# A second modulation on VectorE alone: weights laid with outputs on partitions, one multiply-and-add-up step for each column of outputs

## The chip, the cores and the metric

The kernel runs on one core of one Trainium2 chip (trn2). The core has TensorE (matrix products into PSUM), VectorE, ScalarE, GpSimd, SyncE (which here only issues DMAs), an on-chip memory of 128 partitions (SBUF), and PSUM in eight banks of 512 fp32 columns. The engines run their own instruction streams and wait for one another through semaphores. The metric is the device time of one execution in microseconds (us); lower is better.

## The reference

Two transformer blocks run one after the other on 512 tokens of width 1024, all in fp32. What matters here is the first lines of the first block: a condition vector `c` gives, by one product with a 1024 x 6144 matrix, the six vectors that shift, scale and gate both halves of the block.

```python
s_lat = jax.nn.silu(c)                                   # c: (1, 1024)
mod_l = (s_lat @ w_mod[l] + b_mod[l])[:, None, :]        # w_mod: (1024, 6144)
sh1, sc1, g1, sh2, sc2, g2 = jnp.split(mod_l, 6, axis=-1)
h = _modulate(_rms(x, norm1_g[l]), sh1, sc1)             # needs sh1, sc1 at once
p = h @ w_in[l]                                          # queries, keys, Fourier input, gates ga, gb
...
x = x + g1 * _merge(p, attn_lat, four_lat, ...)          # g1 much later
h2 = _modulate(_rms(x, norm2_g[l]), sh2, sc2)            # sh2, sc2 before the experts
x = x + g2 * _expert_choice(h2, *moe_w)
```

`sh1` and `sc1` are the first modulation. The other four vectors, 4096 outputs of 1024 products each (16 MB of weights), are the second modulation, and are needed only from the merge after the attention on.

## The kernel before

Channels lie on the 128 partitions in 8 groups (KD), tokens along the free axis. A projection tile is one PSUM bank: 128 outputs by 512 tokens, over 8 groups of inputs. Each product is made of three passes (L988 to L990, function `mm3`): both factors are split into a high part (`w_hi`, `h_hi`) and the rest (`w_lo`, `h_lo`), and high x high, high x low and low x high are added up in PSUM. So a tile is 24 matrix products.

Weights come as one stream of chunks, [128, 2048] fp32, 1 MB each. SyncE loads them in a fixed order into a ring of four `raw` slots (L804, L832 to L842). Split chunks are converted by ScalarE (`w_hi`, L1817) and then by GpSimd in two halves (`w_lo`, L918 and L920) into a ring of three; the last of these steps frees the raw slot (`w_lo_done`). A refill waits until the chunk four places before it is done with, and the refills wait in order, so one late slot holds the whole ring. The first section (s1) has 19 split chunks of 16 blocks of 128 x 128 weights, numbered 0 to 18; TensorE takes its blocks in order: queries, keys, Fourier, then gates `ga` (blocks 115 to 178) and `gb` (179 to 242), then `four_o`. Chunk 11 starts at block 176, the sixth block of tile ga 7.

The 16 chunks of the second modulation (raw chunks, not split) are put into this stream by `MOD_BEHIND`: one behind each of split chunks 8 and 9, two behind each of 10 to 16. A chunk holds two groups of 128 outputs, with inputs on the partitions: for output group m and input group k a 128 x 128 block. VectorE works through it in `modulation_b` (L2259): the first step (L2269) scales the k = 0 blocks by the condition (one number for each partition, `csil`), seven more (L2271) multiply and add on, each over 2 x 128 elements, with the running sum in PSUM bank 7; the last writes it into `macc` in SBUF and frees the raw slot (`macc_done`). What is left is a sum over partitions. TensorE does that in `mod_b_tile` (L1020): two products with `macc` as weights and a column of ones, in one of six turning PSUM banks; `mod_b_evac` (L2254) on VectorE adds the bias and writes two columns of `mod`. These tiles stand in TensorE's hand-written order behind ga 4 to 7, gb 0 to 7 and four_o 0 to 3 (L1217 to L1238).

VectorE starts on the second modulation when it is done with the rotated and normalised query rows (`q_rows`, L2443), which also free the PSUM banks for the `ga` tiles. `mod` is first needed (`modb_done`, L1400) at the router logits after the attention.

Of the kernel before, what the change touches and what calls it, by code (L numbers as in the profile page):

```python
# [8 lines left out]
ALU = mybir.AluOpType  # L9
# [279 lines left out]
def make_plan():  # L289
# [37 lines left out]
    for j in range(KD):  # L327
        p.add("ga", j, by="act", split=blocks(s1, S1_GA + j * 8 * B, 8))
        if j >= 4:
            p.add("mod_b", j - 4, by=("modb_done", j - 3))  # L330
    for j in range(KD):
        p.add("gb", j, by="act", split=blocks(s1, S1_GB + j * 8 * B, 8))
        p.add("mod_b", 4 + j, by=("modb_done", 5 + j))
# [4 lines left out]
    for j in range(KD // 2):  # L338
        four_o(j)
        p.add("mod_b", 12 + j, by=("modb_done", 13 + j))  # L340
# [158 lines left out]
def build(nc, stream, cols_d, x_d, ctx_d, router_d, wab_d, rope_t_d, dftc_d, ident_d, iota_d, xt_d, out):  # L499
    with ExitStack() as ctx:  # L500
# [76 lines left out]
        macc = at("macc", R + 104, [P, 4, 2, B])  # L577
# [96 lines left out]
        def ex(m):  # L674
# [28 lines left out]
        macc_done = sem("macc_done")  # L703
# [78 lines left out]
                   "modb_done": modb_done, "silu_e": silu_e, "act_t_done": act_t_done,  # L782
# [18 lines left out]
        def _(sp):  # L801
# [30 lines left out]
            def refill(n):  # L832

                split, k = CHUNKS[n - NRAW]
                if split:
                    sp.wait_ge(w_lo_done, k + 1)
                else:
                    sp.wait_ge(macc_done, k + 1)
# [119 lines left out]
        def _(pe):  # L958
# [52 lines left out]
            def mod_tile(g):  # L1011
# [6 lines left out]
                done(last)  # L1018

            def mod_b_tile(k):  # L1020

                o = open_tile("mod_b", k)
                pe.wait_ge(macc_done, k + 1)
                for m in range(2):
                    last = mm(o[:, m:m + 1], macc[:, k % 4, m, :], one, start=True, stop=True)  # L1025
# [210 lines left out]
            for j in range(KD // 2):  # L1236
                four_out(j)
                mod_b_tile(12 + j)  # L1238
# [561 lines left out]
        def _(act):  # L1800
# [102 lines left out]
            for g in range(NF):  # L1903
                hi(f_hi[:, g, :], take("f", g))
            for g in range(NF + 1):
# [7 lines left out]
                if g >= 1:  # L1913
# [5 lines left out]
                    hi(f_hi[:, g - 1, :], four_f[:, g % 2, :])  # L1919
            for half in range(2):  # L1920
# [298 lines left out]
        def _(dve):  # L2219
# [34 lines left out]
            def mod_b_evac(k):  # L2254
                m = 16 + 2 * k
                V.tensor_tensor(mod[:, m:m + 2, 0], take("mod_b", k)[:, 0:2], col("b_mod", m, 2), ALU.add)\
                    .then_inc(modb_done, 1)

            def modulation_b(c):  # L2259
# [3 lines left out]
                if c < 2:  # L2263
                    dve.wait_ge(qtok_done, 2 * TT)
                else:
                    dve.wait_ge(macc_done, c - 1)
                w = raw[:, n % NRAW, :].rearrange("p (m k c) -> p m k c", m=2, k=KD)
                acc = psum[:, 7, c % 2 * 2 * B:(c % 2 + 1) * 2 * B].rearrange("p (m c) -> p m c", m=2)
                link(V.tensor_scalar(acc, w[:, :, 0, :], csil[:, 0:1], None, ALU.mult))  # L2269
                for k in range(1, KD):  # L2270
                    ins = V.scalar_tensor_tensor(out=acc if k < KD - 1 else macc[:, c % 4, :, :], in0=w[:, :, k, :],  # L2271
                                                 scalar=csil[:, 2 * k:2 * k + 1], in1=acc, op0=ALU.mult, op1=ALU.add)
                    if k < KD - 1:
                        link(ins)
                ins.then_inc(macc_done, 1)

# [196 lines left out]
            for c in range(5, 12):  # L2473
                mod_b_evac(c)
                if c + 4 < 16:
                    modulation_b(c + 4)
# [7 lines left out]
            for j in range(KD // 2):  # L2484
                four_gate(j)
                mod_b_evac(12 + j)
# [641 lines left out]
```

## Time and profile before

| what | us |
|---|---|
| median of 3 runs | 1310.37 (1309.72 to 1312.95) |
| the profiled execution's own time | 1308.97 |
| its span, first to last instruction | 1307.2 |
| TensorE busy in the span | 1290.0 |
| VectorE busy | 675.6 |
| ScalarE busy | 472.1 |
| GpSimd busy | 447.4 |
| mean granted TensorE clock | 0.995 of full |

The profile is of one execution. PE is TensorE, DVE VectorE, ACT ScalarE, POOL GpSimd, SP SyncE. A busy TensorE need not be at its peak: matrix products overlap, and their ends are modelled, so the distance between two starts says more than a duration. Idle time of an engine that nothing waits for costs nothing. The second modulation lies between 149 and 235 us.

### The profile page before, as it was taken

The page shows a single profiled execution, that of the slowest core. Times are in us where ns is not written, and L with a number is a line of the kernel's source. Part 1 is how long each engine was busy: PE and PEld are TensorE (multiplying, and loading weights), DVE is VectorE, ACT ScalarE, POOL GpSimd, SP SyncE. Part 2 cuts the span into 40 slices and gives each one's busy share as a digit, 9 for nine tenths or more (in the row PEclk, how much of TensorE's full clock was granted, in tenths as well). Part 3 has the DMA queues.
Part 4 walks back from the last instruction along what each step waited for, and adds up shares of the span by engine and source line. Part 5 has one row for each costly group of instructions (what it writes and reads, how often), then busy time and mean ns, then how long its engine had stood idle before and what let it go on. Part 6 is the DMA issues. An engine that isn't in the chain of part 4 may idle for free.

```text
span 1307.2 us, 15683 instructions
## 1 busy us (share of the span) xinstructions
PE 1290.0 (99%) x6240; PEld 951.9 (73%) x6240; DVE 675.6 (52%) x1262; ACT 472.1 (36%) x640; POOL 447.4 (34%) x215
## 2 busy tenths in 40 slices
PE   8999999999999999999999999999999999999998
PEld 5789888866588734443357788888888888888887
DVE  2467987668873634342258557422551551551553
ACT  4354232356541312111154661433431431431443
POOL 3153254157630100000035243544254444444440
PEclk9999999999999899999999999999999999999999
DMA  9522298201027899999963221332123223223101
GB/s 374 226 98 97 99 355 303 80 3 63 33 101 298 316 423 420 420 420 420 421 262 119 96 98 65 108 118 97 60 102 123 72 97 124 69 96 125 68 1 65
DMA packets 33764, 226.54 MB, mean 173 GB/s; under 512 B 3872, under 2 KB 4512, under 8 KB 7712
## 3 DMA queue, kind: packets, MB, share of 16 engines
q1 hardware_dynamic: 32256, 218.79, 43.4%
q0 software_dynamic: 1152, 4.19, 0.9%
q10 hardware_dynamic: 288, 2.62, 0.5%
q8 instruction: 46, 0.75, 0.2%
q14 instruction: 22, 0.18, 0.0%
HBM read 221.40 MB, written 4.19 MB: 173 GB/s over the span
## 4 chain that ended last, share of the span: by engine, by line
PE 93%; DMA 3%; DVE 2%; ACT 1%; issue 0%; POOL 0%; SPq 0%; DVEq 0%
PE psum L988 24%; PE psum L989 23%; PE psum L990 23%; PE psum L1531 11%; DMA ex_more<-in_stream 2%; PE psum L1302 2%; PE psum L1273 1%; DMA x<-in_x 1%; PE psum L1616 1%; PE psum L1491 1%; PE psum L1516 1%; DVE x L2613 1%; PE psum L1519 0%; PE psum L1007 0%; PE psum L1025 0%; PE psum L1258 0%
## 5 line engine op out<-in xcount | busy, mean ns | idle before, releaser
L918 POOL TENSOR_TENSOR w_lo<-raw,w_hi 128x1024 fp32r<-128x1024 f32 x79 | 190.4, 2410 | 569.0 <-ACT w_hi L1817 567.6
L988 PE MATMUL psum<-b_hi,w_hi 128*128 128x512 f32 x608 | 238.1, 392 | 0.1
L990 PE MATMUL psum<-b_hi,w_lo 128*128 128x512 f32 x608 | 236.7, 389 | 0.0
L989 PE MATMUL psum<-b_lo,w_hi 128*128 128x512 f32 x608 | 236.6, 389 | 0.0
L1817 ACT ACTIVATE w_hi<-raw 128x2048 fp32r<-128x2048 f32 x80 | 152.6, 1907 | 143.2 <-PE psum L990 101.9
L920 POOL TENSOR_TENSOR w_lo<-raw,w_hi 128x1024 fp32r<-128x1024 f32 x79 | 191.3, 2422 | 0.0
L988 PEld LDWEIGHTS psum<-b_hi,w_hi 128*128 128x128 f32 x608 | 114.1, 188 | 30.8 <-issue 5.7
L990 PEld LDWEIGHTS psum<-b_hi,w_lo 128*128 128x128 f32 x608 | 114.1, 188 | 24.1
L989 PEld LDWEIGHTS psum<-b_lo,w_hi 128*128 128x128 f32 x608 | 114.2, 188 | 23.1
L1531 PE MATMUL psum<-ex_ring,xe 128*64 128x512 f32 x432 | 95.0, 594 | 0.0
L2611 DVE TENSOR_TENSOR x<-psum,x 128x512 f32<-128x512 f32 x39 | 26.9, 692 | 127.7 <-PE psum L990 127.7
L988 PE MATMUL psum<-h_hi,w_hi 128*128 128x512 f32 x200 | 81.1, 406 | 1.3 <-POOL w_lo L900 1.3
L990 PE MATMUL psum<-h_hi,w_lo 128*128 128x512 f32 x200 | 78.2, 391 | 0.0
L989 PE MATMUL psum<-h_lo,w_hi 128*128 128x512 f32 x200 | 78.0, 390 | 0.0
L988 PE MATMUL psum<-ff_hi,w_hi 128*128 128x512 f32 (+1 forms) x198 | 75.9, 383 | 0.0
L990 PE MATMUL psum<-ff_hi,w_lo 128*128 128x512 f32 (+1 forms) x198 | 75.7, 383 | 0.0
L989 PE MATMUL psum<-ff_lo,w_hi 128*128 128x512 f32 (+1 forms) x198 | 75.7, 383 | 0.0
L2927 DVE TENSOR_TENSOR psum<-psum,rstd_s 128x512 f32<-128x512 f32 x48 | 33.5, 697 | 77.4 <-PE psum L990 77.4
L1531 PEld LDWEIGHTS psum<-ex_ring,xe 128*64 128x64 f32 x432 | 30.3, 137 | 59.0 <-issue 58.6
L930 POOL DMA_INDIRECT xg<-xt,ids x8 | 9.2, 1152 | 180.8 <-PE psum L1519 127.1
L2613 DVE SCALAR_TENSOR_TENSOR x<-psum,mod,x 128x512 f32<-128x512 f32 x72 | 50.5, 744 | 26.4 <-PE psum L990 20.1
L2810 DVE TENSOR_TENSOR act_r<-psum,gate_s 128x512 f32<-128x512 f32 x8 | 5.5, 692 | 86.2 <-PE psum L1531 86.2
(463 smaller groups left out, 2349.0 us busy)
## 6 DMA issues: line engine op xcount, KB each, us to landing
raw<-in_stream SPq DMA_DIRECT2D x97, 1024.0 KB, 4.8
ex_ring<-in_stream SPq DMA_DIRECT2D x78, 1024.0 KB, 20.4
ex_more<-in_stream SPq DMA_DIRECT2D x18, 1024.0 KB, 21.6
mod_in<-in_stream SPq DMA_DIRECT2D x8, 1024.0 KB, 20.8
x<-in_x SPq DMA_DIRECT2D x4, 512.0 KB, 6.5
x<-in_x ACTq DMA_DIRECT2D x1, 2048.0 KB, 7.5
xt<-h2t SPq DMA_DIRECT2D x8, 256.0 KB, 9.5
out<-y_out SPq DMA_DIRECT2D x4, 512.0 KB, 3.0
```

Of the source, the lines that this page charges most:

```text
L918: nc.gpsimd.tensor_tensor(w_lo[:, slot, w], raw[:, raw_slot, w], w_hi[:, slot, w].bitcast(F32), ALU.subtract)
L920: nc.gpsimd.tensor_tensor(w_lo[:, slot, w], raw[:, raw_slot, w], w_hi[:, slot, w].bitcast(F32), ALU.subtract).then_inc(w_lo_done, 1)
L988: mm(o, w[0], x[0], start=start, stop=False)
L989: mm(o, w[0], x[1], start=False, stop=False)
L990: return mm(o, w[1], x[0], start=False, stop=stop)
L1273: done(mm(o[:, 0:KH], q_hi[b][0:QK, q * P:(q + 1) * P], k_hi[b][0:QK, s * KH:(s + 1) * KH], start=True, stop=True))
L1302: last = mm(psum[s * VD:s * VD + VD, 6 + h % 2, :], v[:, k + s, h * VD:h * VD + VD], probs[k + s][:], start=k == 0, stop=k == KT - 2)
L1531: last = mm(o[e * CAP:(e + 1) * CAP, :], x_of(k, e), w[:, (2 * (k - k0) + e) * T:(2 * (k - k0) + e + 1) * T], start=k == 0, stop=k == ks - 1)
L1817: A(w_hi[:, c % NHL, :], raw[:, n % NRAW, :], ACT.Copy).then_inc(w_hi_done, 1)
L2611: ins = V.tensor_tensor(x1[:, j, :], o, x1[:, j, :], ALU.add)
L2613: ins = V.scalar_tensor_tensor(out=x1[:, j, :], in0=o, scalar=scale, in1=x1[:, j, :], op0=ALU.mult, op1=ALU.add)
L2927: V.tensor_tensor(o, o, rstd, ALU.mult).then_inc(ffz_done, 1)
```

## The change

The chunks of the second modulation are laid out anew on the host: outputs on partitions, and along the free axis the 1024 weights of each output; a chunk still holds two groups of 128 outputs. The condition is loaded once as a [128, 1024] array with the same row on every partition (`c_rows`), and ScalarE takes its silu there. VectorE then does each group of 128 outputs in one step that multiplies by this row, adds up along the free axis, starts from the bias, and writes one column of `mod`. The `mod_b` tiles of TensorE, their evacuation and `macc` go. `c_rows` takes the place of `macc` in SBUF; `k_rows` lies in the same bytes before, so the load waits for the `kr` tile that reads it.

```diff
 # plan: no mod_b tiles
     for j in range(KD):
         p.add("ga", j, by="act", split=blocks(s1, S1_GA + j * 8 * B, 8))
-        if j >= 4:
-            p.add("mod_b", j - 4, by=("modb_done", j - 3))
...
-        macc = at("macc", R + 104, [P, 4, 2, B])
+        c_rows = at("c_rows", R + 104, [P, D])
...
 # SyncE, refill of a slot that held a modulation chunk
-                    sp.wait_ge(macc_done, k + 1)
+                    sp.wait_ge(modb_done, k + 1)
...
 # TensorE
             for j in range(KD):
                 done(project(open_tile("ga", j), s1, S1_GA + j * 8 * B, B, ks, hx))
-                if j >= 4:
-                    mod_b_tile(j - 4)
             for j in range(KD):
                 done(project(open_tile("gb", j), s1, S1_GB + j * 8 * B, B, ks, hx))
-                mod_b_tile(4 + j)
...
 # ScalarE
             for g in range(NF):
                 hi(f_hi[:, g, :], take("f", g))
+                if g == 2:
+                    full(act, "kr")
+                    act.dma_start(c_rows[:], c_rows_d).then_inc(c_rows_in, 16)
...
+            act.wait_ge(c_rows_in, 16)
+            A(c_rows[:], c_rows[:], ACT.Silu).then_inc(c_rows_done, 1)
...
 # VectorE, modulation_b(c)
-                w = raw[:, n % NRAW, :].rearrange("p (m k c) -> p m k c", m=2, k=KD)
-                acc = psum[:, 7, c % 2 * 2 * B:(c % 2 + 1) * 2 * B].rearrange("p (m c) -> p m c", m=2)
-                link(V.tensor_scalar(acc, w[:, :, 0, :], csil[:, 0:1], None, ALU.mult))
-                for k in range(1, KD):
-                    ins = V.scalar_tensor_tensor(out=acc if k < KD - 1 else macc[:, c % 4, :, :], in0=w[:, :, k, :],
-                                                 scalar=csil[:, 2 * k:2 * k + 1], in1=acc, op0=ALU.mult, op1=ALU.add)
...
+                w = raw[:, n % NRAW, :].rearrange("p (m i) -> p m i", m=2)
+                for i in range(2):
+                    m = 16 + 2 * c + i
+                    ins = V.tensor_tensor_reduce(out=w[:, i, :], in0=w[:, i, :], in1=c_rows[:], scale=1.0, scalar=col("b_mod", m),
+                                                 op0=ALU.mult, op1=ALU.add, accum_out=mod[:, m, 0:1])
+                ins.then_inc(modb_done, 1)
...
             for half in range(2):
                 q_sums(half)
                 q_rows(half)
-            for c in range(4):
-                modulation_b(c)
-            for c in range(5):
-                mod_b_evac(c)
-                modulation_b(c + 4)
...
+            dve.wait_ge(c_rows_done, 1)
+            for c in range(16):
+                modulation_b(c)
```

TensorE's order, at the end of tile ga 4, before:

```order
678 L989 MATMUL psum<-h_lo,w_hi 128x512
679 L990 MATMUL psum<-h_hi,w_lo 128x512
680 L1025 MATMUL psum<-ones,macc 128x1 [waits macc_done,qtok_done]
681 L1025 MATMUL psum<-ones,macc 128x1
682 L988 MATMUL psum<-h_hi,w_hi 128x512 [waits freed_act]
683 L989 MATMUL psum<-h_lo,w_hi 128x512
```

and now (the three passes have lines 985 to 987 in the changed file):

```order
678 L986 MATMUL psum<-h_lo,w_hi 128x512
679 L987 MATMUL psum<-h_hi,w_lo 128x512
680 L985 MATMUL psum<-h_hi,w_hi 128x512 [waits qtok_done]
681 L986 MATMUL psum<-h_lo,w_hi 128x512
682 L987 MATMUL psum<-h_hi,w_lo 128x512
```

The two one-column products and their wait for VectorE are gone; ga 5 follows ga 4 directly.

VectorE's order, from the last step of the query rows on, before (`small` holds the condition's silu, one number for each partition):

```order
193 L2462 TENSOR_TENSOR q_tok_111<-q_tok_111,r_q 128x4x32
194 L2269 TENSOR_SCALAR psum<-raw,small 128x256 [waits qtok_done,raw_full1]
195 L2271 SCALAR_TENSOR_TENSOR psum<-raw,small,psum 128x256 [waits dve_seq] x6
196 L2271 SCALAR_TENSOR_TENSOR macc<-raw,small,psum 128x256 [waits dve_seq]
197 L2269 TENSOR_SCALAR psum<-raw,small 128x256 [waits qtok_done,raw_full3]
198 L2271 SCALAR_TENSOR_TENSOR psum<-raw,small,psum 128x256 [waits dve_seq] x6
```

and now (ISA is the multiply-and-add-up step, and behind it the readout of the sum into a column of `mod`):

```order
193 L2439 TENSOR_TENSOR q_tok_111<-q_tok_111,r_q 128x4x32
194 L2251 ISA raw,mod<-raw,c_rows,cols 128x1024 [waits raw_full1,c_rows_done]
195 L2251 ISA mod 128x1
196 L2251 ISA raw,mod<-raw,c_rows,cols 128x1024
197 L2251 ISA mod 128x1
198 L2251 ISA raw,mod<-raw,c_rows,cols 128x1024 [waits raw_full3]
```

Eight steps for a chunk have become two with their readouts; the operands `raw` and `c_rows` are both in SBUF, where the second tensor was in PSUM.

ScalarE's order at the end of the Fourier stage, now (before, the rows are the same but for row 62):

```order
59 L1812 ACTIVATE f_hi<-four_f 128x512 [waits four_done]
60 L1903 ACTIVATE four_sin<-psum 128x256 [waits tile_full]
61 L1812 ACTIVATE f_hi<-four_f 128x512 [waits four_done]
62 L1909 ACTIVATE c_rows<-c_rows 128x1024 [waits c_rows_in]
63 L1802 ACTIVATE w_hi<-raw 128x2048 [waits raw_full0,tile_full]
64 L1916 ACTIVATE sqs_q<-psum 128x384 [waits tile_full] x2
65 L1916 ACTIVATE sqs_q<-psum 128x384 [waits qsum_done,tile_full] x6
```

The silu of `c_rows` has been put ahead of a weight split and of the squares of the query rows, without a table load beside it.

## Rows read from the trace of the kernel before

**Rows 1.** The page, busy time (us, share of the span) and instructions.

```profile
PE 1290.0 (99%) x6240; PEld 951.9 (73%) x6240; DVE 675.6 (52%) x1262; ACT 472.1 (36%) x640; POOL 447.4 (34%) x215
```

**Rows 2.** TensorE's waits for a weight split: us in total, times, longest.

```profile
PE psum L988 <- POOL w_lo L900: 1.3, 2, 0.9
```

**Rows 3.** Timeline of TensorE, first products behind each tile: start us, us.

```profile
144.80 0.39 PE L988 MATMUL psum<-h_hi,w_hi 128*128 128x512 f32 x1
...
150.24 0.39 PE L988 MATMUL psum<-h_hi,w_hi 128*128 128x512 f32 x1
...
155.68 0.50 PE L1025 MATMUL psum<-ones,macc 128*128 128x1 f32 x4
...
161.63 0.50 PE L1025 MATMUL psum<-ones,macc 128*128 128x1 f32 x4
```

**Rows 4.** Two stretches: length, busy us of each engine, clock, DMA share, GB/s.

```profile
150.00:235.00 85.00, 85.00 (x405) 70.85 (x404) 64.90 (x147) 21.08 (x21) 33.27 (x14) 1.00 0.83 309
...
525.00:660.00 135.00, 133.31 (x625) 54.70 (x622) 46.79 (x81) 22.08 (x47) 2.80 (x3) 1.00 1.01 421
```

**Rows 5.** VectorE, timeline of modulation chunk 0; last, line 2271's durations (ns).

```profile
149.20 0.49 DVE L2269 TENSOR_SCALAR psum<-raw,small 128x256 f32<-128x256 f32 x1
...
152.87 0.48 DVE L2271 SCALAR_TENSOR_TENSOR macc<-raw,small,psum 128x256 f32<-128x256 f32 x1
153.27 0.48 DVE L2269 TENSOR_SCALAR psum<-raw,small 128x256 f32<-128x256 f32 x1
...
L2271 DVE SCALAR_TENSOR_TENSOR psum<-raw,small,psum x96: 487/490/491, 149.7 to 224.9; 128x256 f32<-128x256 f32 x96
```

**Rows 6.** Timelines: chunk 11's conversion, TensorE's use, chunk 12's last half.

```profile
164.32 1.92 ACT L1817 ACTIVATE w_hi<-raw 128x2048 fp32r<-128x2048 f32 x1 [13.28 <-DMA raw<-in_stream]
...
168.66 2.40 POOL L920 TENSOR_TENSOR w_lo<-raw,w_hi 128x1024 fp32r<-128x1024 f32 x1
...
171.48 0.39 PE L988 MATMUL psum<-h_hi,w_hi 128*128 128x512 f32 x1
...
177.30 2.40 POOL L920 TENSOR_TENSOR w_lo<-raw,w_hi 128x1024 fp32r<-128x1024 f32 x1
```

**Rows 7.** SyncE, timeline: the refills from modulation chunk 0's release on.

```profile
153.38 4.87 SPq L805 DMA_DIRECT2D raw<-in_stream  x4
```

**Rows 8.** VectorE, groups by form: busy us, mean ns of one, idle.

```profile
L2940 DVE TENSOR_TENSOR ff_pre<-acc_u,ff_gl 128x512 f32<-128x512 f32 x24 | 16.6, 692 | 0.8
...
L2658 DVE SCALAR_TENSOR_TENSOR b_lo<-x,cols,b_hi 128x512 fp32r<-128x512 f32 x16 | 12.0, 750 | 0.8 <-ACT b_hi L1827 0.3
...
L2902 DVE TENSOR_TENSOR_SCAN lru_v<-lru_a,lru_b 128x512 f32<-128x512 f32 x8 | 11.9, 1484 | 0.3
...
L2511 DVE TENSOR_TENSOR k_tok<-kr_tok,r_k 128x256 f32<-128x256 f32 x6 | 2.5, 416 | 0.0
...
L2256 DVE TENSOR_TENSOR mod<-psum,cols 128x2 f32<-128x2 f32 x16 | 2.5, 154 | 5.7 <-PE psum L1025 5.7
```

**Rows 9.** Timelines: GpSimd's split steps and VectorE's steps on SBUF operands.

```profile
142.04 2.39 POOL L918 TENSOR_TENSOR w_lo<-raw,w_hi 128x1024 fp32r<-128x1024 f32 x1 [1.50 <-ACT w_hi L1817]
...
142.52 2.06 DVE L2462 TENSOR_TENSOR q_tok<-q_tok,r_q 128x128 f32<-128x128 f32 x1
...
114.93 2.10 DVE L2234 TENSOR_TENSOR f_lo<-four_f,f_hi 128x512 fp32r<-128x512 f32 x1 [0.77 <-ACT f_hi L1827]
...
116.44 2.86 POOL L920 TENSOR_TENSOR w_lo<-raw,w_hi 128x1024 fp32r<-128x1024 f32 x1
```

**Rows 10.** ScalarE 1024 wide; timelines around the first query rows and ga 0.

```profile
L1864 ACT ACTIVATE w_hi<-raw x1: 1057/1057/1057, 18.4 to 18.4; 128x1024 fp32r<-128x1024 f32 x1
...
122.40 0.49 ACT L1926 ACTIVATE sqs_q<-psum 128x384 f32<-128x384 f32 x1 [0.56 <-PE psum L990]
...
127.77 0.28 DVE L2462 TENSOR_TENSOR q_tok<-q_tok,r_q 128x128 f32<-128x128 f32 x1
...
128.44 0.39 PE L988 MATMUL psum<-h_hi,w_hi 128*128 128x512 f32 x1
```

More of the change, by code:

```diff
@@ L328, in make_plan @@
         p.add("ga", j, by="act", split=blocks(s1, S1_GA + j * 8 * B, 8))
-        if j >= 4:
-            p.add("mod_b", j - 4, by=("modb_done", j - 3))
     for j in range(KD):
         p.add("gb", j, by="act", split=blocks(s1, S1_GB + j * 8 * B, 8))
-        p.add("mod_b", 4 + j, by=("modb_done", 5 + j))
     def four_o(j, bank=None):
@@ L339, in make_plan @@
         four_o(j)
-        p.add("mod_b", 12 + j, by=("modb_done", 13 + j))
     for t in range(KT):
@@ L496, with build @@
 FFN_CHUNKS = 9
-def build(nc, stream, cols_d, x_d, ctx_d, router_d, wab_d, rope_t_d, dftc_d, ident_d, iota_d, xt_d, out):
+def build(nc, stream, cols_d, x_d, ctx_d, router_d, wab_d, rope_t_d, dftc_d, ident_d, iota_d, c_rows_d, xt_d, out):
     with ExitStack() as ctx:
@@ L702, in build @@
         cpad_zero = sem("cpad_zero")
-        macc_done = sem("macc_done")
+        c_rows_in = sem("c_rows_in")
+        c_rows_done = sem("c_rows_done")
         modb_done = sem("modb_done")
@@ L781, in build @@
                    "pre_done": pre_done, "accg_done": accg_done, "accu_done": accu_done,
-                   "modb_done": modb_done, "silu_e": silu_e, "act_t_done": act_t_done,
+                   "silu_e": silu_e, "act_t_done": act_t_done,
                    "rcol_done": rcol_done, "lru_b_done": lru_b_done, "gcol_done": gcol_done}
@@ L1017, in mod_tile @@
                               start=True, stop=True)
[L1018 to L1025, printed above, removed]
                 done(last)
@@ L1237, in _ @@
                 four_out(j)
-                mod_b_tile(12 + j)
             def token_rows(o, t, off):
@@ L2252, in mod_evac @@
                 dve.wait_ge(freed_dve, PLAN.freed_count(TILE["mod", g]))
[L2254 to L2257, printed above, removed]
             def modulation_b(c):
@@ L2467, in _ @@
                 q_rows(half)
-            for c in range(4):
+            dve.wait_ge(c_rows_done, 1)
+            for c in range(16):
                 modulation_b(c)
-            for c in range(5):
-                mod_b_evac(c)
-                modulation_b(c + 4)
[L2473 to L2476, printed above, removed]
             def four_gate(j):
@@ L2485, in _ @@
                 four_gate(j)
-                mod_b_evac(12 + j)
             V.memset(k_hi[0][QK:QK + 1, :].bitcast(F32), 1.0)
@@ L3033 @@
              for q in range(4) for base in (0, D) for k in range(KD)]
-    mod = tiles(w_mod)[:, 8 * CH:]
+    mod = w_mod[:, 2 * D:].T.reshape(-1, P, D).transpose(1, 0, 2).reshape(P, -1)
     w_in = a["w_in"][0]
@@ L3118 @@
               "rope_t": rope_t, "dftc": dftc, "ident": np.eye(P, dtype=f),
-              "iota": np.ascontiguousarray(iota)}
+              "iota": np.ascontiguousarray(iota),
+              "c_rows": np.ascontiguousarray(np.broadcast_to(a["c"][0].reshape(1, D), (P, D)))}
     nc = bacc.Bacc("TRN2", target_bir_lowering=False, num_devices=1)
```

7 lines of the change are left out of this document (removed).

## The prediction

> **What bounds the kernel now.** I read the busy shares first. TensorE is busy 1290.0 of 1307.2 us [rows 1], so a change counts only as far as it removes TensorE work or makes TensorE wait. TensorE's list of waits comes next: no weight chunk is waited for after the first one [rows 2] (L900 is the first chunk's split alone). Then the table by stretches: in 150 to 235 us, where the second modulation runs, TensorE is busy all 85.00 us at granted clock 1.00 (2.4 GHz), VectorE 64.90 and GpSimd 33.27 us, and the DMA engines carry 309 GB/s [rows 4]. So the stretch is TensorE's, with three suppliers close behind, and these have to be followed one by one.
>
> **What goes from TensorE.** A plain projection tile, 24 matrix products, takes 150.24 - 144.80 = 5.44 us from start to start. With a mod_b tile behind it the period is 161.63 - 155.68 = 5.95 us [rows 3]. One mod_b tile (two one-column products, in the trace four) therefore costs 0.51 us, more than its columns suggest, since the products behind it start slowly as well. Sixteen of them, the last four behind shorter tiles but of the same form: 8.1 us, all on the path.
>
> **What goes from and comes to VectorE.** Before, a chunk takes 153.27 - 149.20 = 4.07 us: eight steps of 256 elements in a chain [rows 5]. Now it takes two multiply-and-add-up steps of 1024 elements, each followed by a readout of one column (the piece of VectorE's order, now). The trace has no such step, so I bound it. A two-input step on SBUF operands takes 692 ns for 512 elements and 416 for 256, that is 1.08 ns for one element, hence 692 + 512 x 1.08 = 1.24 us for 1024 [rows 8]. Its successor starts 0.08 us before its recorded end, as in rows 5 (0.48 us long, next start 0.40 later). So T = 1.16 us, or 1.2 by the three-input form (750 ns). The upper end is the scan, also a running result over two inputs: 1484 ns for 512 [rows 8], so up to 2.97 us. The lower end is 1.11 us, the slope alone. I take 1.16, because the form is that of the two-input step and the scan feeds each result into the next product, while a sum does not have to; the readout I take as 0.1 us, between nothing and the 0.15 us of a step on two columns [rows 8]. A chunk is then 2 x 1.26 = 2.5 us, and VectorE has 16 x 1.5 = 24 us less to do; that by itself is off the path and worth nothing.
>
> The Trainium skill speaks against this change. "Vector Engine (DVE) Microarchitecture Reference", section "Points that are easy to get wrong", says that this family of steps runs at half throughput with two SBUF sources that aren't bf16, as no read port is left for the accumulator. The rows show 750 ns for such a step with two fp32 SBUF sources and 512 elements [rows 8], which is no halving; but that step adds nothing up, so the rule isn't refuted. By the rule a step would take some 2.3 us and the kernel about 1327 us (rival 2, worked out there from rows), by the row 1.2 and 1303.
>
> **The weight ring.** A raw slot is handed back when its modulation chunk is done, and SyncE's queue refills in order. The row of SyncE at 153.38 is the refill that waited for mod chunk 0; it and three more go out within 4.87 us [rows 7]. The third of them is weight chunk 11 of the first section, and ScalarE starts on it at 164.32 [rows 6], 10.9 us after 153.38: three transfers of 1.05 MB at 309 GB/s [rows 4] are 10.2 us. So this burst is held by the DMA rate, and only its start can be moved. GpSimd ends the chunk's low part at 168.66 + 2.40 = 171.06, and TensorE first uses it at 171.48 (tile ga 7, block 5) [rows 6]. That is a cushion of 0.42 us, which the waits list doesn't show. After the change three mod_b tiles fewer stand ahead of it, so TensorE wants it at 171.48 - 1.53 = 169.95. VectorE is done with chunk 0 at 149.20 + 2.5 = 151.7 instead of 153.3, so the burst starts 1.6 us earlier: ScalarE starts at 162.7, GpSimd at 164.7. Without more, the low part would be ready at 169.4, in time.
>
> **The shared port.** Here the new step's operands count. The old steps had their second tensor in PSUM, and all 96 took 487 to 491 ns [rows 5], whatever GpSimd did. Steps of VectorE with both tensors in SBUF don't: one of 128 elements, started at 142.52, ends at 144.58 with GpSimd's step 142.04 to 144.43; the other way round GpSimd's step from 116.44 takes 2.86 us instead of 2.40, as VectorE's from 114.93 had waited and held it until 117.03 [rows 9]. So they exclude one another, and a waiting VectorE step goes first at the change-over. (The Trainium skill, "SBUF — State Buffer", section "Who interferes with whom", has this as a lock held for the whole instruction when VectorE has two SBUF inputs and GpSimd reads SBUF; by that rule each of the 32 new steps can block half a weight split. The trace agrees.) Mod chunk 4 is the fourth transfer of the burst and lands at about 165, inside GpSimd's first half (164.7 to 167.1). Its first step waits until 167.1 and runs to 168.3; GpSimd's second half follows, to 170.7. TensorE, wanting it at 169.95, waits 0.8 us.
>
> Behind that the ring has room. One round is a weight chunk of 16 blocks, 2 x 5.44 = 10.9 us of TensorE, and holds two mod chunks and one split. With everything on the port in turn it needs 4 x (T + 0.1) + 4.7 = 9.7 us. Chunk 12 was ready at 177.30 + 2.40 = 179.7 [rows 6] with TensorE's need at 171.48 + 2 x 5.95 = 183.4; after, the need is 181.6 (five tiles fewer, 0.8 later), and the split starts about 1.6 us earlier, takes up to two steps (2.4 us) more, and is ready at about 180.5. I see no second wait.
>
> **The added conversion of the condition.** The DMA (0.5 MB) goes out behind the third f tile and is wanted behind the last Fourier tile, with the whole Fourier stage in between; covered. The Silu over 1024 elements takes about 1.0 us by the nearest row (1057 ns) [rows 10]; no table load stands with it in its order. It stands ahead of a split and of the squares of the query rows. Of these, the fourth waited for TensorE 0.56 us [rows 10], and VectorE's sums follow it, so some 0.4 us of the 1.0 reach the query rows. VectorE frees the first bank at 127.77 + 0.28 = 128.05, and TensorE takes it at 128.44 [rows 10]: the 0.4 us use up that cover, and 0.1 us may show. Later the same lag vanishes: the step from 142.52 waits for GpSimd until 144.4 anyway [rows 9], so modulation still starts at 149.2. Were that cover gone, the first wait grows by the 0.4.
>
> The PSUM banks turn over in another order without mod_b, but each bank still comes back after six tiles (33 us) until the fixed ones. mod is needed at the logits, hundreds of us later.
>
> **Sum.** -8.1 + 0.8 + 0.1 = -7.2 us. The profiled execution took 1308.97 us (span 1307.2, 1.8 around it), 1.4 below the median of 1310.37. So its counterpart is 1301.8, and the median forecast 1303.2. Without the lock it would be -8.1; with T of 1.45 chunk 11 comes 1.5 to 2 us late, and it is about -6.
>
> **The rivals.**
> 1. *The forecast*, 1303.2 (1302 to 1305): 0.65.
> 2. *Two cycles for one element.* T is then 0.14 + 2 x 1.08 x 1024 ns = 2.35 us, and a round needs 4 x 2.45 + 4.7 = 14.5 us against 10.9. The burst starts 0.8 us later, GpSimd begins at 167.1 and, with two steps of 2.35 in between, ends at 176.5: chunk 11 is 6.5 us late. The rounds of chunks 13 to 17 lose 3.6 each (that of 12 lies in the first wait): 6.5 + 18 - 8.1 = +16.4, about 1327 us. At the scan's 2.97 a round loses 6.0 and the time is about 1341. It decides from T = 1.45, where the round is full; at about 1.8 us the whole gain is gone. For it: the scan's row. Against it: the sum needs no feedback. 0.10.
> 3. *The lock costs more than one step*, by T of 1.5 to 1.7, by a readout that takes the port too, or by GpSimd losing each turn: waits of 1 to 3 us at chunk 11 and about 1 at later chunks, gain 1 to 5 us, about 1307. 0.15.
> 4. *The gain is given back in the expert stage*, where the DMA engines are busy to a share of 1.01 from 525 to 660 us [rows 4]. For it: a stream that ran from a fixed time would end when it did. Against it: it starts on slots that TensorE's progress frees, so it starts as much earlier. 1310. 0.08.
> 5. The rest, 0.02: something else, of either sign.
>
> What can be told from no change is 0.3%, 3.9 us, so 1306.4 and 1314.3 are the bounds. Case 1 and half of case 3 are faster: 0.73. Half of case 3, case 4 and a little of 5 are the same: 0.16. Case 2 and the rest are slower: 0.11. The range 1301.5 to 1309 takes in case 1 and most of case 3, about 0.8; the likeliest case's own range is 1302 to 1305.
>
> **What would show it.** Right: a step of 1.2 to 1.3 us x32 on VectorE; tile periods of 5.44 us through gb; a single wait of TensorE for a weight split, 0.3 to 1.5 us long near 170 us; some GpSimd halves of 3.5 us instead of 2.4; everything behind 235 us earlier by one amount. Wrong: steps above 1.45 us, waits on the splits at every second or third tile, or a shift at 235 us that is smaller by 650 us.

## The result, and the profile after

| | before | after |
|---|---|---|
| median, us (4 runs each, alternating on one chip) | 1310.05 (1309.65 to 1312.95) | 1301.09 (1299.18 to 1302.03) |
| profiled execution, us | 1308.97 | 1301.71 |
| its span | 1307.2 | 1299.9 |
| mean granted TensorE clock | 0.995 | 0.996 |

The ratio is 0.992 (0.9907 to 0.9934): faster by 9.0 us. Forecast were 7.2 us and 1303.2 us, with a range from 1301.5. The direction and the main term were right; the time lies 0.4 us below the range.

The page after, busy time (compare [rows 1]):

```profile
PE 1282.9 (99%) x6176; PEld 945.6 (73%) x6176; DVE 671.2 (52%) x1182; ACT 473.3 (36%) x641; POOL 453.3 (35%) x215
```

TensorE is busy 7.1 us less, with 64 products fewer, and still 99% of the span. The stretch of the second modulation (length, busy us of each engine, clock, DMA share, GB/s; compare [rows 4]):

```profile
150.00:235.00 85.00, 85.00 (x376) 70.25 (x375) 67.54 (x80) 25.19 (x26) 45.48 (x16) 1.00 0.81 310
525.00:660.00 135.00, 131.70 (x614) 53.34 (x611) 42.77 (x73) 23.69 (x48) 6.53 (x4) 1.00 1.01 421
```

TensorE is still busy throughout. VectorE is shown busy 67.54 us where it was 64.90, though its work was to fall by some 24 us, and GpSimd 45.48 where it was 33.27. Part of this is work of the next stage that now falls into the window: 16 halves of weight splits on GpSimd instead of 14, and some 6 us more on VectorE. The rest is told by the groups and the timelines. VectorE's groups from 145 to 245 us (busy us, mean ns of one, idle before):

```profile
L2251 DVE CUSTOM_DVE_ANT_0 raw<-raw,c_rows,cols 128x1024 f32<-128x1024 f32 x32 | 58.3, 1872 | 11.5 <-DMA raw<-in_stream 11.5
...
L2251 DVE DVE_READ_ACCUMULATOR2_ANT mod<- 128x1 f32 x32 | 2.5, 78 | 0.0
```

VectorE's timeline (start us, us), first where GpSimd is idle, then at modulation chunk 4:

```profile
150.23 1.28 DVE L2251 CUSTOM_DVE_ANT_0 raw<-raw,c_rows,cols 128x1024 f32<-128x1024 f32 x1
151.44 0.08 DVE L2251 DVE_READ_ACCUMULATOR2_ANT mod<- 128x1 f32 x1
151.44 1.28 DVE L2251 CUSTOM_DVE_ANT_0 raw<-raw,c_rows,cols 128x1024 f32<-128x1024 f32 x1
...
165.03 3.05 DVE L2251 CUSTOM_DVE_ANT_0 raw<-raw,c_rows,cols 128x1024 f32<-128x1024 f32 x1 [2.47 <-DMA raw<-in_stream]
168.01 0.07 DVE L2251 DVE_READ_ACCUMULATOR2_ANT mod<- 128x1 f32 x1
168.01 3.41 DVE L2251 CUSTOM_DVE_ANT_0 raw<-raw,c_rows,cols 128x1024 f32<-128x1024 f32 x1
```

GpSimd's timeline over the same chunks:

```profile
164.60 2.40 POOL L915 TENSOR_TENSOR w_lo<-raw,w_hi 128x1024 fp32r<-128x1024 f32 x1 [17.32 <-ACT w_hi L1802]
166.96 3.37 POOL L917 TENSOR_TENSOR w_lo<-raw,w_hi 128x1024 fp32r<-128x1024 f32 x1
173.50 2.59 POOL L915 TENSOR_TENSOR w_lo<-raw,w_hi 128x1024 fp32r<-128x1024 f32 x1 [3.17 <-ACT w_hi L1802]
```

By itself the step takes 1.28 us and the next starts 1.21 us after it; the readout (0.08 us) lies beside the next step. The step that starts at 165.03 takes 3.05 us, since GpSimd's half, 164.60 to 167.00, is under way; GpSimd's second half then takes 3.37 us instead of 2.40, as VectorE goes first at the change-over; and VectorE's next step, begun inside that half, takes 3.41. Both engines are shown busy while they wait for each other. In e3 below, where they don't, the same 32 steps are busy 39.6 us instead of 58.3. So 18.7 us of VectorE's time here is waiting.

ScalarE starts on chunk 11 of the first section, and TensorE uses it (two timelines; compare [rows 6]):

```profile
162.60 1.92 ACT L1802 ACTIVATE w_hi<-raw 128x2048 fp32r<-128x2048 f32 x1 [11.13 <-DMA raw<-in_stream]
```

```profile
170.17 0.39 PE L987 MATMUL psum<-h_hi,w_lo 128*128 128x512 f32 x1
170.40 0.48 PE L985 MATMUL psum<-h_hi,w_hi 128*128 128x512 f32 x1
170.72 0.40 PE L986 MATMUL psum<-h_lo,w_hi 128*128 128x512 f32 x1
```

GpSimd is done at 166.96 + 3.37 = 170.33, and TensorE takes the chunk at 170.40, where its turn comes anyway. TensorE's list has no wait for a split in this stretch; the next product starts 0.32 us later instead of 0.23, and this 0.1 us is all that the chunk costs.

ScalarE starts 1.72 us earlier than before (162.60 for 164.32). The refill behind modulation chunk 0 goes out only 0.63 us earlier, and the other 1.1 us come behind it. SyncE's refills before, each line with two, and the DMA engines (last two numbers: share, GB/s) between 160 and 162 us:

```profile
153.38 0.80 SPq L805 DMA_DIRECT2D raw<-in_stream  x2
157.44 0.81 SPq L805 DMA_DIRECT2D raw<-in_stream  x2
160.00:162.00 2.00, 2.00 (x13) 1.69 (x12) 1.90 (x4) 0.00 (x0) 0.00 (x0) 1.00 0.80 250
```

and after:

```profile
152.75 0.80 SPq L802 DMA_DIRECT2D raw<-in_stream  x2
155.17 0.80 SPq L802 DMA_DIRECT2D raw<-in_stream  x2
160.00:162.00 2.00, 2.00 (x10) 1.67 (x9) 2.00 (x5) 0.00 (x0) 0.00 (x0) 1.00 0.98 414
```

The third refill, chunk 11's, waits for VectorE to hand back modulation chunk 1. With 4.07 us for a chunk it goes out at 157.44, and the DMA rate has a gap at 160 us; with 2.42 us it goes out at 155.17, and there is no gap.

A sharper measure than the windows is how much later or earlier the same product of TensorE starts, taken over all its products in order, without the one-column ones. The first product on the latent keys starts here in the kernel before and in the kernel after:

```profile
234.37 0.49 PE L988 MATMUL psum<-w_hi,ckv_hi 128*128 128x512 f32 x1
```

```profile
226.95 0.39 PE L985 MATMUL psum<-w_hi,ckv_hi 128*128 128x512 f32 x1
```

They are 7.42 us apart. The same difference at other places, against the kernel before's first profile (us; b1_before is a second profile of the kernel before, a1_after one more of the kernel after):

| at (before's time) | after | a1_after | b1_before |
|---|---|---|---|
| 150 | +0.44 | +0.46 | +0.51 |
| 240 | -7.56 | -7.48 | +0.51 |
| 420 | -7.49 | -7.55 | +0.43 |
| 450 | -7.85 | -9.02 | +0.79 |
| 700 | -7.24 | -8.10 | +1.47 |

Between 150 and 240 us both profiles of the kernel after gain 7.9 to 8.0 us. The second execution of the kernel before is 0.5 us later from 20 us on, and 1.5 us later at 700.

### The profile page after: what moved, and what is told of

Its sections match the earlier page's. It is cut to its first block, busy times and chain, and to the rows that moved or that the text cites. A ratio compares the mean times of both kernels' runs of the same rounds, so it can differ in the third digit from the quotient of the medians.

```text
span 1299.9 us, 15446 instructions
## 1 busy us (share of the span) xinstructions
PE 1282.9 (99%) x6176; PEld 945.6 (73%) x6176; DVE 671.2 (52%) x1182; ACT 473.3 (36%) x641; POOL 453.3 (35%) x215
## 4 chain that ended last, share of the span: by engine, by line
PE 93%; DMA 4%; DVE 2%; SPq 1%; ACT 0%; issue 0%; DVEq 0%
PE psum L985 24%; PE psum L986 23%; PE psum L987 23%; PE psum L1516 11%; DMA ex_more<-in_stream 2%; PE psum L1287 2%; DMA mod_in<-in_stream 2%; PE psum L1258 1%; PE psum L1601 1%; DVE x L2583 1%; PE psum L1476 1%; PE psum L1501 0%; PE psum L1504 0%; PE psum L1243 0%; PE psum L1029 0%; PE psum L1004 0%
## 5 line engine op out<-in xcount | busy, mean ns | idle before, releaser
L915 POOL TENSOR_TENSOR w_lo<-raw,w_hi 128x1024 fp32r<-128x1024 f32 x79 | 192.0, 2430 | 555.7 <-ACT w_hi L1802 554.3
L917 POOL TENSOR_TENSOR w_lo<-raw,w_hi 128x1024 fp32r<-128x1024 f32 x79 | 197.2, 2496 | 0.0
L2251 DVE CUSTOM_DVE_ANT_0 raw<-raw,c_rows,cols 128x1024 f32<-128x1024 f32 x32 | 58.3, 1872 | 11.5 <-DMA raw<-in_stream 11.5
```

What stands on the lines that cost most here:

```text
L915: nc.gpsimd.tensor_tensor(w_lo[:, slot, w], raw[:, raw_slot, w], w_hi[:, slot, w].bitcast(F32), ALU.subtract)
L917: nc.gpsimd.tensor_tensor(w_lo[:, slot, w], raw[:, raw_slot, w], w_hi[:, slot, w].bitcast(F32), ALU.subtract).then_inc(w_lo_done, 1)
L2251: ins = V.tensor_tensor_reduce(out=w[:, i, :], in0=w[:, i, :], in1=c_rows[:], scale=1.0, scalar=col("b_mod", m), op0=ALU.mult, op1=ALU.add ...
```

## The experiments

**The kernel after once more, and the columns back.** a1_after is the kernel after without an edit. e1_columns_back adds at each of the 16 places:

```diff
+            def column_products():
+                pe.wait_ge(qtok_done, 2 * TT)
+                for m in range(2):
+                    mm(psum[:, 7, 510 + m:511 + m], ident[:], one, start=True, stop=True)
```

> The changed kernel as it is, timed again beside the kernel before, to size the gain. Theory A (only TensorE's sixteen column tiles count): 16 x 0.505 = 8.1 us go, a wait of 0.1 for weight chunk 11 and 0.1 for the late first query rows come: 8.0 us faster, ratio 0.9939, and the 9.0 us of the first comparison are partly scatter between executions. Theory B (something behind 235 us gives another us, in the expert stage or by the clock): 9 us or more again, ratio 0.9932 or less.

> The changed kernel with two one-column products put back at each of the sixteen places in TensorE's order; they multiply the identity by a column of ones into a spare corner of bank 7, nothing waits for them and nothing reads them. Theory A: the whole gain goes, within 0.5 us of the kernel before (ratio 0.9995 to 1.0005). Theory B, or a gain that comes from VectorE's shorter work: it stays at least 1 us faster.

Measured: a1_after 1301.29 (1300.68 to 1301.54), ratio 0.9919 (0.9906 to 0.9932). e1_columns_back 1312.10 us, ratio 1.000 (0.9992 to 1.0009). By its time a1_after speaks for theory B, as it is 10.2 us faster than the kernel before in the same comparison; in the stage it gains the 8.0 us of theory A. What lies between is taken up at the end. Against the profile after, e1's later products start 0.08 us later at 150 and 8.07 at 235, in steps of 0.5 us. With the 32 short products back (64 in the trace), and VectorE, GpSimd and the ring as after, the whole gain is gone. The gain is TensorE's time; e9 below shows what VectorE's shorter work adds.

**How many columns.** The same with one product (e7) and four (e8) at each place.

```diff
-                for m in range(2):
+                for m in range(1):      # e8: range(4), columns 508 to 511
```

> The kernel after, with one one-column product (instead of two) at each of the 16 places where a mod_b tile stood; its result is not used. Two cost 0.50 us for each place by the shift of TensorE's later products (8.07 us for 16). Theory A, each product pays for itself (its own weights have to be brought in, and one column is too short to hide that): about 0.25 us a place, 4 us in all, 1305.3 us. Theory B, the cost is that of breaking into the run of 512-column products, whatever stands there: 0.4 to 0.45 us a place, 6.5 to 7 us, about 1308 us.

> The same with four one-column products at each of the 16 places. Theory A: about 1.0 us a place, 16 us in all, so about 1317 us, unless the suppliers' added time hides nothing (TensorE is the bound there, so all of it shows). Theory B: 0.6 to 0.7 us a place, 10 to 11 us, about 1312 us.

Measured: e7 1305.77 us, ratio 0.9953 (0.9936 to 0.9969); e8 1316.49 us, ratio 1.0039 (1.0027 to 1.005). The shift from 150 to 235 us was 3.83 us (0.24 a place) for one product, 7.99 (0.50) for two and 15.14 (0.95) for four. Timeline of TensorE in e8:

```profile
156.13 0.95 PE L1210 MATMUL psum<-ones,ident 128*128 128x1 f32 x8
156.94 0.49 PE L985 MATMUL psum<-h_hi,w_hi 128*128 128x512 f32 x1
157.27 0.40 PE L986 MATMUL psum<-h_lo,w_hi 128*128 128x512 f32 x1
157.50 0.40 PE L987 MATMUL psum<-h_hi,w_lo 128*128 128x512 f32 x1
```

The four (eight in the trace) hold the engine for 156.94 - 156.13 = 0.81 us, and the product behind them is followed after 0.33 instead of 0.23 us. The price grows with the number of products, about 0.24 us for each fp32 product of one column. That is theory A's count; its reason, the weights that each product brings in, was not tested by itself. A pass of 512 columns has a pitch of 5.44 / 24 = 0.23 us, so a one-column product costs about as much.

**Before without the tiles.** VectorE keeps its eight steps; the sum over partitions is left out. In e2 the small step that writes `mod` reads `macc` in SBUF; e9 reads PSUM instead for chunks 0 to 11.

```diff
-                mod_b_tile(j - 4)            # and at the other 12 places
...
-                V.tensor_tensor(mod[:, m:m + 2, 0], take("mod_b", k)[:, 0:2], ...)
+                dve.wait_ge(macc_done, k + 1)
 # e2
+                V.tensor_tensor(mod[:, m:m + 2, 0], macc[:, k % 4, :, 0], ...)
 # e9
+                part = psum[:, 7, (k + 1) % 2 * 2 * B:(k + 1) % 2 * 2 * B + 2] if k < 12 else macc[:, k % 4, :, 0]
+                V.tensor_tensor(mod[:, m:m + 2, 0], part, ...)
```

> The kernel before with the mod_b tiles taken from TensorE and nothing else: VectorE still does eight steps a chunk, and its evacuation takes one column of the running sums instead of their sum over partitions (that sum is left out, so the modulation's values are other ones). Theory A: -8.1 us for the tiles, but weight chunk 11 is ready at 171.1 as before and wanted at 169.95: a wait of 1.1 us appears for it, so 7.0 us faster, ratio 0.9947, 1 us less than the changed kernel. If VectorE's shorter work is worth nothing at all: 8.1 faster and no wait.

> Before without the sixteen mod_b tiles, like e2_no_tiles (the sum over partitions is left out), but the small step that writes two columns of mod has its first operand in PSUM for chunks 0 to 11, as the old evacuation had. In e2_no_tiles both its operands lay in SBUF, and it took 1131 ns on average instead of 154 (18.1 us instead of 2.5), so VectorE there had some 15 us more to do than before the change. Theory A, the 2.7 us between e2 and the kernel after were an artefact of these steps: about 1301.5 us, and TensorE waits neither for gbf nor for the split by more than 0.5 us near 230 us. Theory B, VectorE's eight steps for each chunk are themselves too long once TensorE runs 8 us ahead: about 1303 to 1304 us with waits of 1.5 to 3 us left at that place.

Measured: e2 1304.04 us (1302.38 to 1307.18), ratio 0.994 (0.9926 to 0.9955); e9 1303.29 (1301.33 to 1306.15), ratio 0.9944 (0.9931 to 0.9958). TensorE's waits in 145 to 245 us (us in total, times, longest), in e2 and then in e9:

```profile
PE psum L984 <- DVE gbf L2475: 2.6, 2, 2.2
PE psum L984 <- POOL w_lo L916: 1.0, 1, 1.0
```

```profile
PE psum L984 <- POOL w_lo L916: 0.9, 1, 0.9
```

And VectorE's group that differs, in e2:

```profile
L2249 DVE TENSOR_TENSOR mod<-macc,cols 128x2 f32<-128x2 f32 x16 | 18.1, 1131 | 0.0
```

A step on two columns takes 1131 ns on average there against 154 ns with an operand in PSUM [rows 8], since half of them start beside one of GpSimd's halves and wait for its end (0.15 us alone, 1.25 to 2.39 us beside one). That delays VectorE until TensorE waits for `gbf`. So e2 was spoilt in part by its own edit. In e9 the wait for `gbf` is gone and one of 0.9 us is left, at chunk 11; the shift from 150 to 240 us is -6.9 against -8.0 for the whole change. This is what VectorE's shorter work is worth, 0.9 us of waiting and 1.1 in the shift: with the long steps ScalarE takes chunk 11 at 164.41, as before, and with the short ones at 162.60, and the chunk comes in time. At the end of the stage, where theory B expected waits, there are none, yet the time is the one of theory B. By the medians e9 is 2.2 us behind the kernel after, but its runs scatter over 4.8 us, so about 1 us is shown and the rest isn't explained.

**The port, with the row in PSUM.** ScalarE copies the silu of the row into PSUM banks 6 and 7 when they are free, behind ga 2, and the step reads it there.

```diff
+                if j == 2:                       # ScalarE, behind ga 2
+                    act.wait_ge(qtok_done, 2 * TT)
+                    A(c_ps, c_rows[:], ACT.Copy).then_inc(c_rows_done, 1)
...
-                        in1=c_rows[:], ...
+                        in1=c_ps, ...
```

> The changed kernel with the condition's row copied by ScalarE into PSUM banks 6 and 7 behind the query rows, and read from there. Theory of the shared port: all 32 steps take 1.28 us and all split halves of GpSimd 2.4 (none of 3.4), where now steps of 2 to 3.4 us and halves of 3.4 stand. As that lock costs TensorE only 0.1 us at chunk 11 in the changed kernel, the time is the same within 0.3 us. If the lock costs more than the trace's waits show (rival 3): 0.5 to 1 us faster than the changed kernel.

Measured: 1302.34 us, ratio 0.9929 (0.9916 to 0.9941). VectorE's group and GpSimd's in 145 to 245 us:

```profile
L2256 DVE CUSTOM_DVE_ANT_0 raw<-raw,psum,cols 128x1024 f32<-128x1024 f32 x32 | 39.6, 1279 | 25.8 <-DMA raw<-in_stream 24.7 <-ACT psum L1923 1.2
```

```profile
L918 POOL TENSOR_TENSOR w_lo<-raw,w_hi 128x1024 fp32r<-128x1024 f32 x9 | 21.7, 2408 | 0.0
L916 POOL TENSOR_TENSOR w_lo<-raw,w_hi 128x1024 fp32r<-128x1024 f32 x8 | 19.2, 2399 | 48.8 <-ACT w_hi L1803 48.8
```

Every step takes 1.28 us and every half 2.40: with one of VectorE's two tensors in PSUM the engines don't exclude each other, and VectorE's busy time falls from 58.3 to 39.6 us. (The Trainium skill, "SBUF — State Buffer", section "Who interferes with whom", names two SBUF inputs as the condition; e3 is the counterpart to the kernel after, and agrees.) Yet the time doesn't fall; it is 1.05 us above that of a1_after. The edit has a price of its own: VectorE waits 1.16 us for ScalarE's copy and starts on the modulation at 150.80. Chunk 11 is ready at 167.55 + 2.40 = 169.95 and is used at 170.01, 0.28 us behind its turn. So e3 doesn't price the exclusion exactly. What bounds its cost in the kernel after is that kernel's own timeline, 0.1 us at chunk 11: the rest was inside the suppliers' slack.

e3 also tells what held the burst. Its first refill goes out at 153.32, as before the change (153.38), and with the short steps ScalarE has chunk 11 at 163.20 all the same, 1.1 us sooner than before.

**The same work twice.** Each step is done twice, which gives steps of about 2.5 us, first with both tensors in SBUF (e4), then with the row in PSUM (e5).

```diff
+                    link(V.tensor_tensor_reduce(out=c_ps, in0=w[:, i, :], in1=c_rows[:], ...,   # e4
+                                                accum_out=mod[:, m, 1:2]))
                     ins = V.tensor_tensor_reduce(out=w[:, i, :], in0=w[:, i, :], in1=c_rows[:], ...)
 # e5: out=c_rows and in1=c_ps in the first, in1=c_ps in the second
```

> The changed kernel with each of VectorE's 32 steps done twice, the first time with its product put into PSUM banks 6 and 7 and its sum into an unused column; both tensors that it reads are in SBUF. So a mod chunk costs four steps of 1.21 us, as if T were 2.4 (rival 2's price). With the port shared, a round (one weight split, two mod chunks) needs 8 x 1.25 + 4.7 = 14.7 us against TensorE's 10.9, so TensorE waits 4 to 5 us for chunk 11 and then 3 to 4 us for each of chunks 13 to 17: about 16 us slower than the kernel before (10 to 20). If the port is no constraint: like e5.

> The same doubling with the condition's row in PSUM (banks 6 and 7) and the first product put into SBUF, so no step reads two tensors from SBUF. VectorE has the same work as in e4_twice, but no lock against GpSimd: a round needs 10 us for VectorE and 4.7 for GpSimd side by side, within 10.9. Theory of the shared port: split halves of 2.4 us, one wait of 1 to 3 us at chunk 11 and perhaps one at the end, when four_gate stands behind the last mod chunk; 4 to 7 us faster than the kernel before, some 20 us faster than e4_twice. If VectorE's length alone counts: as slow as e4_twice.

Measured: e4 1339.86 us (1338.61 to 1340.09), ratio 1.0212 (1.0197 to 1.0228); e5 1309.02 us, ratio 0.9981 (0.9971 to 0.999). The same number of steps differs by 31 us. The added step writes to PSUM in e4 and to SBUF in e5, which makes a pair 2.60 instead of 2.54 us where GpSimd is idle, some 0.2 us in a round; the rest is the exclusion and what follows from it. TensorE's waits in e4, then in e5:

```profile
PE psum L986 <- POOL w_lo L918: 17.0, 5, 4.9
PE psum L986 <- DVE gbf L2457: 13.9, 1, 13.9
```

```profile
PE psum L986 <- POOL w_lo L918: 4.0, 1, 4.0
```

GpSimd's rounds in e4:

```profile
196.47 3.10 POOL L916 TENSOR_TENSOR w_lo<-raw,w_hi 128x1024 fp32r<-128x1024 f32 x1 [10.59 <-ACT w_hi L1803]
...
210.79 3.17 POOL L916 TENSOR_TENSOR w_lo<-raw,w_hi 128x1024 fp32r<-128x1024 f32 x1 [7.95 <-ACT w_hi L1803]
...
225.23 3.12 POOL L916 TENSOR_TENSOR w_lo<-raw,w_hi 128x1024 fp32r<-128x1024 f32 x1 [7.98 <-ACT w_hi L1803]
```

A round takes 14.3 to 14.4 us against the 10.9 that TensorE needs. Rival 2 had computed 14.5 for just these steps, with chunk 11 late by 6.5 us and 3.6 lost in each of five rounds behind it. Measured are waits of 4.9 us for chunk 11 and of 4.0, 1.7, 3.2 and 3.2 behind it. What it had missed is the end. VectorE's queue has the product of `gbf` behind the last chunk, and TensorE waits 13.9 us for it. On top comes the clock. Windows of e4 and of e5:

```profile
246.00:270.00 24.00, 9.99 (x30) 7.50 (x31) 22.36 (x29) 5.30 (x5) 12.05 (x5) 0.57 0.66 254
```

```profile
170.00:185.00 15.00, 11.02 (x36) 8.81 (x37) 14.82 (x24) 3.01 (x4) 8.69 (x4) 0.77 0.77 283
```

From 246 to 270 us, around and behind the long wait, the granted clock is 0.57 of 2.4 GHz on average: most of it at 1.2 GHz. In e5 the clock falls to 1.2 GHz at 173.2, near the end of its single wait, and is back at 180.0. The wait of 4.0 us and 6 us of work at half clock (3 lost) give the shift of 7.1 us at 180 us, and from there to 240 it grows by only 0.4: without the exclusion a round is 8 x 1.27 = 10.2 us of VectorE, under 10.9. Forecast was a wait of 1 to 3 us and 4 to 7 us less than the kernel before; with the longer wait and the clock it became 2.5 us less.

**ScalarE's silu earlier.** It goes into ScalarE's idle time before the last `f_hi`.

```diff
+                    if g == NF:                 # behind the last four_sin
+                        act.wait_ge(c_rows_in, 16)
+                        A(c_rows[:], c_rows[:], ACT.Silu).then_inc(c_rows_done, 1)
...
-            act.wait_ge(c_rows_in, 16)          # behind the last f_hi
-            A(c_rows[:], c_rows[:], ACT.Silu).then_inc(c_rows_done, 1)
```

> The changed kernel with the silu of the condition's row put into ScalarE's idle time of 2.7 us ahead of the last f_hi, instead of behind it. Nothing but the 0.1 us by which tile ga 0 starts late should come back: the first query rows are free 0.6 us earlier, tile ga 0 starts on time, and the time is the changed kernel's within 0.3 us. If the silu costs more than the trace shows: 0.5 us or more faster.

Measured: 1301.28 us (1301.04 to 1301.83), ratio 0.9921 (0.9907 to 0.9934), the same as after. In its trace the silu, 1.05 us from 114.86, lies in idle time, and between 40 and 150 us TensorE gains 0.10 us on the kernel after (its shift goes from -0.48 to -0.58). That is the 0.1 us of the forecast, too small to see in a time. More changes for the suppliers: the modulation starts at 148.87 instead of 150.23, though TensorE is only 0.6 us ahead, and chunk 11 is ready at 165.56 + 3.38 = 168.94 and used at 169.82. The 0.1 us that it costs in the kernel after is gone too (the shift goes on to -0.69).

**The kernel before once more,** to see what differs between executions.

> The kernel before as it is, for a second profile. The profiled execution of before that the prediction was made against took 1308.97 us, less than every timed one (1310.0 to 1314.1). If scatter between executions is what makes 8.0 us of the matched profiles into 9 to 10 of the medians: a profile of about 1310 to 1313, with the difference between 415 and 460 us, where the clock is halved for a while, or in the first 25 us; the stretch from 150 to 240 us alike within 0.1.

Measured: 1310.45 us, span 1308.6; its shifts stand in the table above.

## Where the prediction was right, and where it failed

**The tiles, -8.1 us: right.** TensorE's products behind the stage start 7.9 to 8.0 us earlier in both profiles, and e1 gives back 7.99 of it for the 16 places.

**The step, 1.16 us and 0.1 for the readout: right within 5%.** Measured are 1.21 from start to start, with a readout that costs nothing, so a chunk takes 2.42 us (forecast 2.5). The Trainium skill, "Vector Engine (DVE) Microarchitecture Reference", section "Points that are easy to get wrong", has half the rate for the form S2S2D2_STT with two SBUF sources that aren't bf16; an estimate by that is 2.3 us, and the row shows 1.28 with both tensors fp32 in SBUF. The trace names this step CUSTOM_DVE_ANT_0 and not SCALAR_TENSOR_TENSOR, so it shows that this step isn't halved, and leaves open whether the rule holds for the other. Rival 2 falls with it. e4, which makes such steps by doubling, took 1339.86 us where that rival had 1327, as `gbf` and the clock were not in its sum.

**The wait for chunk 11: the term that failed.** The forecast had 0.8 us. Measured is none that the waits list shows, and 0.1 by the timeline; rival 3, with waits of 1 to 3 us, falls with it. The turns at the port came as forecast: chunk 4's first step waited, and GpSimd's second half of chunk 11 came after it. The step that was wrong stands ahead of them, "this burst is held by the DMA rate, and only its start can be moved". It was worked out with 309 GB/s, the mean of an 85 us stretch with gaps in it. In the burst itself the engines carry 414 to 434 GB/s (156 to 165 us in the kernel after), and what held chunk 11 before was VectorE: its refill waited for modulation chunk 1 (157.44). With the shorter steps the way from the first refill to ScalarE's start takes 9.85 us instead of 10.94. e3 (9.88) and e9 (10.87, with the long steps) show that the steps make the difference.

The other parts of the term, measured against TensorE's own progress (this execution runs 0.44 us late at 150 us): the modulation started 0.6 us later than forecast, the burst took 1.1 us less, and from ScalarE's start to the end of the split it took 7.73 us instead of 8.0. Chunk 11 was thus ready 0.8 us sooner than forecast. That the whole execution ran late doesn't matter here: in e7, which is 0.37 us ahead of the kernel after, the modulation and the chunk are as much ahead. So two errors of 0.6 and 1.1 us partly cancelled, on a cushion of some tenths.

**The late silu: the price right for TensorE, wrong for the modulation.** The prediction let ScalarE's lag vanish in the step from 142.52 and had the modulation start at 149.2. It started at 150.23. VectorE waited for GpSimd twice, as it had before:

```profile
142.52 2.49 DVE L2436 TENSOR_TENSOR q_tok<-q_tok,q_sw 128x128 f32<-128x128 f32 x1
...
145.39 2.03 DVE L2439 TENSOR_TENSOR q_tok<-q_tok,r_q 128x128 f32<-128x128 f32 x1
```

Before, the two took 2.06 us from 142.52 and 1.91 from 145.08. The cover was not there: e6, without the lag, starts the modulation 1.36 us earlier, and only 0.6 of that is TensorE's. The prediction had named this case ("were that cover gone, the first wait grows by the 0.4"); the shorter burst hid it.

**VectorE's 24 us "worth nothing": wrong by about 1 us.** The prediction counted only the earlier start of the burst. Start and burst together brought chunk 11 forward by 1.7 us, and e9 shows that without this TensorE waits 0.9 us for it and gains 1.1 us less.

**The expert stage (rival 4): did not give the gain back.** Between 520 and 660 us, where the DMA engines are busy to 1.01, the shift stays at -7.9 (a1_after: -9.1). Between 660 and 700 us it falls by 0.6, and by 1.0 in a1_after; but b1_before, which is the kernel before, moves by 0.8 the same way, so the change is not what does it.

**From the sum to the median.** In the stage the sum should have been -8.0 instead of -7.2, which would have given 1302.4. That is inside the range, and 1.3 us above the measured 1301.09; 0.3 of it is that the kernel before's median came out at 1310.05 instead of 1310.37. The remaining 1 us is not in the stage, and no term of the sum stands for it. Either of the two, the wait's 0.7 or this 1 us, had to be absent for the time to lie inside the range. That the profiled execution came so near its forecast (1301.8, measured 1301.71) is luck: it has the stage's 0.8 more, and it ran 0.4 us late up to 150 us and lost 0.3 behind 240. The kernel before's medians in five calls were 1310.05, 1311.47, 1311.55, 1310.88 and 1311.75 us, and its profiled 1308.97 is near the lowest of all its runs (1308.29); the kernel after's 1301.71 lies 0.6 above its median. The range's lower end, 1301.5, allowed the tiles' full 8.1 us and 0.8 of anything else, less than the medians of one kernel differ from call to call.

**What stays open.** The medians differ by 9.0 and 10.2 us in two calls, the stage by 8.0. The profiles differ most between 415 and 460 us, where the granted clock is 1.2 GHz for 7 to 14 us in every one, at slightly different times. The window from 420 to 430 us in the kernel after:

```profile
420.00:430.00 10.00, 9.33 (x63) 8.91 (x62) 8.17 (x29) 6.69 (x11) 0.00 (x0) 0.71 0.98 380
```

The total at half clock there was 10.2 us in both profiles of the kernel before, 10.2 and 6.8 in those of the kernel after, and 13.6 in e6. 3.4 us more or less at half clock is 1.7 us of time. In the thirteen profiles it lies between 6.8 and 13.6 us with no order by kernel that could be told. Whether the remaining 1 to 2 us are real, and whether the change shifts them, isn't settled.

## What to carry to other kernels

Where TensorE is never idle, look for its shortest products first: a one-column fp32 product costs about what a pass of 512 columns does, so sixteen pairs were worth 8 us. To tell what holds a burst of transfers, compare the rate within the burst, and the moment of every refill in it, not the mean rate of a long stretch: here the supplier's second release held it, and a faster supplier moved more than the start. Work may be moved from it to an engine that shares a port with another as long as each round of the ring fits with the two taking turns; work out that round (here 9.7 of 10.9 us), since past it each round adds a wait, and slow stretches of the clock come on top (31 us between e4 and e5). A cushion worked out to a few tenths of a microsecond from one execution is uncertain by as much, and the median forecast should carry the scatter of medians on both sides.

## What the runs showed of the hardware

- The multiply-and-add-up step of VectorE on 128 x 1024 fp32 takes 1.28 us, next start after 1.21, whether its second tensor is in SBUF or PSUM; its readout is a record of its own of 0.08 us that lies beside the next step.
- In e4, with the product written to PSUM, the first readout of each pair takes 0.14 us, and the linked step starts 0.18 us after the readout's start instead of with it; in e5, with the product written to SBUF, 0.08 and 0.12 us.
- Small steps are excluded too: steps on two columns with both operands in SBUF took 1.13 us on average in e2, 0.15 where GpSimd was idle and up to 2.39 beside its split (0.15 each with one operand in PSUM).
- With a wait of TensorE of 4.0 us in e5 the clock was halved for 6.8 us, 6 of them behind the wait, worth 3 us more; in e2, where the longest wait was 2.2 us, the window from 220 to 235 us has a clock of 0.89.
- In the burst of refills the DMA engines carry 414 to 434 GB/s between 156 and 165 us of the kernel after; in the kernel before, whose third refill goes out 2.3 us later, it is 250 between 160 and 162.
